# A two-block transformer kernel: constants and vectors ahead of the input, a 72-column slab with its weights stationary

## What is computed

```python
def first_block(x, c, norm_mix_g, w_in, ...):
    mod = silu(c) @ w_ada[l] + b_ada[l]
    sh_m, sc_m, g_m, sh_f, sc_f, g_f = jnp.split(mod, N_MOD, axis=-1)
    h = modulate(rmsnorm(x, norm_mix_g[l]), sh_m, sc_m)
    proj = h @ w_in[l]
    q, k, v, qi, ki, wi, u, ga, gb = jnp.split(proj, split_at, axis=-1)
    ...
    # dsa_attention, per block of queries
    idx_logits = jnp.einsum('btjd,bsd->btjs', qib, k_idx32) * (IDX_DIM ** -0.5)
    score = jnp.einsum('btj,btjs->bts', wb, jax.nn.relu(idx_logits))
    _, sel = lax.top_k(score, topk)
    ...
```

## Time and profile before

| | |
|---|---|
| median of three runs | 979.19 us |
| lowest, highest | 978.38, 985.32 us |
| the profiled execution | 981.8 us |
| its span, first to last instruction | 980.0 us |
| mean granted TensorE clock | 0.994 of full |
| PE, DVE, ACT busy | 95%, 64%, 47% of the span |

### The profile page before, as it was taken

The page is one execution under the profiler, slowest core; times in us unless marked ns, Lnnn a source line. Parts: engine busy times, 40 slices in busy tenths (PEclk is TensorE's granted clock), DMA queues, the critical chain, the costliest instruction groups (busy, mean ns, idle before and its releaser), DMA issues.

```text
span 980.0 us, 12127 instructions
## 1 busy us (share of the span) xinstructions
PE 932.3 (95%) x4313; PEld 749.4 (76%) x4313; DVE 629.6 (64%) x1020; ACT 458.5 (47%) x708; POOL 29.6 (3%) x41
## 2 busy tenths in 40 slices
PE   4799899999999999999999999999999999999997
PEld 4688664578878888887888777788788878888785
DVE  4478899988765555576766534578554565555444
ACT  1144432357364444453744554474455365555432
POOL 2100000000000000000000000000000000000000
PEclk9989999999999999999999999999999999999999
DMA  9977622584566565476565443146462456555531
GB/s 330 338 285 271 216 87 87 174 305 175 168 220 210 172 189 196 171 244 228 164 217 177 129 129 129 43 150 216 143 202 85 130 181 194 183 174 194 188 130 43
DMA packets 102999, 178.05 MB, mean 182 GB/s; under 512 B 6302, under 2 KB 52619, under 8 KB 102954
## 3 DMA queue, kind: packets, MB, share of 16 engines
q1 hardware_dynamic: 96138, 151.23, 46.9%
q0 software_dynamic: 6816, 26.22, 7.3%
HBM read 176.39 MB, written 1.05 MB: 181 GB/s over the span
## 4 chain that ended last, share of the span: by engine, by line
PE 81%; issue 7%; DVE 5%; DMA 3%; ACT 2%; SPq 0%; POOL 0%; DVEq 0%; POOLq 0%; ACTq 0%
PE bank L550 19%; PE bank L552 19%; PE bank L551 19%; PE bank L952 10%; PE bank L583 3%; DMA tap_rows<-in_w_dw 2%; DMA ada_raw<-in_w_ada 2%; PE bank L777 1%; ACT w_hi L1201 1%; DVE w_lo L1660 1%; PE bank L931 1%; PE bank L629 1%; PE bank L793 1%; PE bank L621 1%; PE bank L1146 1%
## 5 line engine op out<-in xcount | busy, mean ns | idle before, releaser
L1660 DVE TENSOR_TENSOR w_lo<-raw_weights,w_hi 128x1024 fp32r<-128x1024 f32 x267 | 324.4, 1222 | 241.5 <-ACT w_hi L1201 240.1
L1201 ACT ACTIVATE w_hi<-raw_weights 128x1024 fp32r<-128x1024 f32 x267 | 281.0, 1058 | 307.7 <-PE bank L552 230.0
L550 PE MATMUL bank<-w_hi,a_hi 128*128 128x512 f32 (+1 forms) x824 | 328.0, 398 | 5.9 <-DVE w_lo L1660 3.3
L552 PE MATMUL bank<-w_hi,a_lo 128*128 128x512 f32 (+1 forms) x824 | 321.0, 390 | 0.0
L551 PE MATMUL bank<-w_lo,a_hi 128*128 128x512 f32 (+1 forms) x824 | 320.6, 389 | 0.0
L550 PEld LDWEIGHTS bank<-w_hi,a_hi 128*128 128x128 f32 x824 | 155.6, 189 | 43.4 <-issue 7.3
L552 PEld LDWEIGHTS bank<-w_hi,a_lo 128*128 128x128 f32 x824 | 155.7, 189 | 32.7
L551 PEld LDWEIGHTS bank<-w_lo,a_hi 128*128 128x128 f32 x824 | 155.9, 189 | 29.9 <-issue 0.2
L952 PE MATMUL bank<-w_hi,ff_hi 128*128 128x512 f32 x176 | 55.1, 394 | 0.8 <-DVE hidden_rows L2162 0.5
L952 PE MATMUL bank<-w_lo,ff_hi 128*128 128x512 f32 x176 | 54.3, 389 | 0.0
L952 PE MATMUL bank<-w_hi,ff_lo 128*128 128x512 f32 x176 | 54.2, 389 | 0.0
(11 more groups left out here) (260 smaller groups left out, 867.4 us busy)
## 6 DMA issues: line engine op xcount, KB each, us to landing
raw_weights<-in_w_in SPq DMA_DIRECT2D x40, 1024.0 KB, 5.1
raw_weights<-in_w_ffn_in SPq DMA_DIRECT2D x44, 512.0 KB, 4.7
raw_weights<-in_w_gate_up SPq DMA_DIRECT2D x44, 512.0 KB, 4.3
ada_raw<-in_w_ada POOLq DMA_DIRECT2D x10, 1024.0 KB, 7.7
ada_start<-in_w_ada POOLq DMA_DIRECT2D x10, 1024.0 KB, 11.5
raw_weights<-in_w_ffn_out SPq DMA_DIRECT2D x9, 1024.0 KB, 4.9
raw_weights<-in_w_down SPq DMA_DIRECT2D x9, 1024.0 KB, 4.9
raw_weights<-in_w_out SPq DMA_DIRECT2D x8, 1024.0 KB, 5.1
```

What stands on the lines that cost most here:

```text
L550: pe.matmul(ps, hi[:, kt, ts], wh, start=start, stop=False)
L552: return pe.matmul(ps, lo[:, kt, ts], wh, start=False, stop=stop)
L1201: act.activation(w_hi[:, slot, 0:m], raw[:, b % RAW, half * PIECE:half * PIECE + m], ACT.Copy)\
L1660: dve.tensor_tensor(w_lo[:, slot, 0:m], raw[:, b % RAW, half * PIECE:half * PIECE + m], w_hi[:, slot, 0:m], ALU.subtract).then_inc(lo_read ...
```

## The change

- SP issues the constants, the eleven vectors and the taps right behind c, and only then waits for ada block 1 and issues x.
- PE transposes the vectors after the first two of its four column batches, and waits there for the constants and the small transfers; its other two column batches and the first sums come behind. DVE copies them out after ada block 2 instead of 6.
- The small slab is computed the other way round: weights stationary (72 columns), activations streaming (256 columns), 24 matmuls instead of 48, into one bank as 72 rows x 256 tokens.
- ACT copies this straight into rows 0 to 71 of kiT. Rows 0 to 63 are the transposed keys. POOL copies them to rows 64 to 127 by a transfer within the chip, which overwrites the weights' rows 64 to 71 once PE has transposed those back into bank 4 (two tiles of 8 columns). DVE scales them from there, as the last thing of slab (1, 3).
- ki_twice, its four copies, two large transposes and one copy of 256 columns are gone.

```diff
@@ SP @@
         sp.dma_start(c_cols[:], ...)
-        sp.wait_ge(*ada_signal(1))
-        sp.dma_start(x[:], ...).then_inc(sem["x_landed"], 16)
         ...
         sp.dma_start(tap_rows[:], ...).then_inc(small_landed, 16)
+        sp.wait_ge(*ada_signal(1))
+        sp.dma_start(x[:], ...).then_inc(sem["x_landed"], 16)
@@ POOL @@
         pool.wait_ge(nt["lo"], 4 * F_OF[N_H1] + 4)
-        for n in range(12, 20):
+        for n in range(12, 14):
+            ada_block(n)
+        pool.wait_ge(sem["wi_turned"], 1)
+        pool.dma_start(kiT[DH:2 * DH, :], kiT[0:DH, :]).then_inc(sem["ki_doubled"], 16)
+        for n in range(14, 20):
             ada_block(n)
@@ PE @@
-        for n in range(4):
+        for n in range(2):
             start_columns(n)
         pe.wait_ge(sem["const_landed"], 16)
-        start_sums(0)
-        start_sums(1)
         pe.wait_ge(small_landed, 16 * 12)
         ...
         last.then_inc(sem["vec_turned"], 1)
+        for n in range(2, 4):
+            start_columns(n)
+        start_sums(0)
+        start_sums(1)
         hold(5, 0)
@@ PE, small slab @@
-        for t in range(TT):
-            for kt in range(KD):
-                last = mm3(bank[2 * (U_SMALL % 2) + t][:, 0:SMALL], kt, t, a_hi, a_lo, sm_hi[:, kt, :],
-                           sm_lo[:, kt, :], kt == 0, kt == KD - 1)
-            if t == 0:
-                last.then_inc(acc_done, 1)
+        out = bank[2 * (U_SMALL % 2)][0:SMALL, 0:SEQ]
+        for kt in range(KD):
+            pe.matmul(out, sm_hi[:, kt, :], a_hi[:, kt, :], start=(kt == 0), stop=False)
+            before = pe.matmul(out, sm_lo[:, kt, :], a_hi[:, kt, :], start=False, stop=False)
+            last = pe.matmul(out, sm_hi[:, kt, :], a_lo[:, kt, :], start=False, stop=(kt == KD - 1))
+        before.then_inc(acc_done, 1)
@@ PE, slabs @@
                 if (s, j) == (1, 2):
-                    pe.wait_ge(sem["ki_copied"], 1)
                     for t in range(TT):
-                        last = pe.transpose(bank[4][:, t * P:(t + 1) * P], ki2[...], ident)
-                    last.then_inc(sem["ki_turned"], 1)
+                        pe.wait_ge(acc_free[t], U_SMALL + 1)
+                        last = pe.transpose(bank[4][:, t * HEADS:(t + 1) * HEADS], kiT[DH:SMALL, t * P:(t + 1) * P],
+                                            ident[DH:SMALL, DH:SMALL])
+                    last.then_inc(sem["wi_turned"], 1)
                 elif (s, j) == (2, 0):
-                    pe.wait_ge(sem["ki_moved"], 1)
+                    pe.wait_ge(sem["wi_scaled"], 1)
                 ...
                     pe.wait_ge(sem["qi_moved"], 2)
+                    pe.wait_ge(sem["ki_doubled"], 16)
                     logits(0, 3)
@@ ACT @@
-            act.wait_ge(*((piece_used, P_SMALL + 1) if t else (acc_done, U_SMALL + 1)))
-            act.activation(z[:, t, C_KI:C_U], bank[2 * (U_SMALL % 2) + t][:, 0:SMALL], ACT.Copy)\
+            act.wait_ge(piece_used, P_SMALL + 1)
+            act.activation(kiT[0:SMALL, t * P:(t + 1) * P], bank[2 * (U_SMALL % 2)][0:SMALL, t * P:(t + 1) * P], ACT.Copy)\
                 .then_inc(acc_free[t], 1)
         ...
-                if (s, k) == (1, 3):
-                    act.wait_ge(sem["ki_turned"], 1)
-                    act.activation(kiT[:], bank[4][:, 0:SEQ], ACT.Copy).then_inc(sem["ki_moved"], 1)
@@ DVE @@
-            elif n == 6:
+            elif n == 2:
                 dve.wait_ge(sem["vec_turned"], 1)
         ...
-                if (s, k) == (1, 0):
-                    ...
-                            last = dve.tensor_copy(ki2[:, t, c, :], z[:, t, C_KI:C_WI])
-                    last.then_inc(sem["ki_copied"], 1)
-                    dve.tensor_scalar(wi_s[:], z[:, :, C_WI:C_U], HEADS ** -0.5, None, ALU.mult)
+                if (s, k) == (1, 3):
+                    dve.wait_ge(sem["wi_turned"], 1)
+                    dve.tensor_scalar(wi_s[:], bank[4][:, 0:TT * HEADS].rearrange("p (t h) -> p t h", t=TT), HEADS ** -0.5,
+                                      None, ALU.mult).then_inc(sem["wi_scaled"], 1)
```

More of the change, by code:

```diff
@@ L213, in build @@
     kiT = sb("kiT", [P, SEQ])
-    ki2 = sb("ki_twice", [P, TT, 2, DH])
     u_at = region(24576)
@@ L381, in _ @@
         sp.dma_start(tap_rows[:], a["w_dw"].rearrange("o t i c -> (o t i) c")).then_inc(small_landed, 16)
+        sp.wait_ge(*ada_signal(1))
+        sp.dma_start(x[:], a["x"].rearrange("o (t p) d -> p (o t) d", p=P)).then_inc(sem["x_landed"], 16)
         def load(b, src, wide=None, i=0, step=0):
@@ L1339, in _ @@
                 conv(P_IN1 + 4 * s + 4 + k)
-                if (s, k) == (1, 3):
-                    act.wait_ge(sem["ki_turned"], 1)
-                    act.activation(kiT[:], bank[4][:, 0:SEQ], ACT.Copy).then_inc(sem["ki_moved"], 1)
-                elif (s, k) == (2, 2):
+                if (s, k) == (2, 2):
                     act.wait_ge(sem["pad_zeroed"], 1)
@@ L1917, in _ @@
                 conv(P_IN1 + 4 * s + 4 + k)
-                if (s, k) == (1, 0):
-                    dve.wait_ge(acc_free[0], U_SMALL + 1)
-                    dve.wait_ge(acc_free[1], U_SMALL + 1)
-                    for t in range(TT):
-                        for c in range(2):
-                            last = dve.tensor_copy(ki2[:, t, c, :], z[:, t, C_KI:C_WI])
-                    last.then_inc(sem["ki_copied"], 1)
-                    dve.tensor_scalar(wi_s[:], z[:, :, C_WI:C_U], HEADS ** -0.5, None, ALU.mult)\
-                        .then_inc(sem["wi_scaled"], 1)
+                if (s, k) == (1, 3):
+                    dve.wait_ge(sem["wi_turned"], 1)
+                    dve.tensor_scalar(wi_s[:], bank[4][:, 0:TT * HEADS].rearrange("p (t h) -> p t h", t=TT), HEADS ** -0.5,
+                                      None, ALU.mult).then_inc(sem["wi_scaled"], 1)
         dve.wait_ge(ada_step, ada_count(6))
```

3 lines of the change are left out of this document (removed).

## The result

The changed kernel takes 972.24 us, the median of seven runs (970.53 to 975.5). The kernel before, in seven runs beside it, has a median of 983.68 (978.38 to 985.32). These seven fall into two groups, two at 978.4 and 979.2 and five from 982.6 to 985.3, so the quotient of the two medians, 0.9884, says little; the ratio recorded for these runs is 0.9913, with a 95% interval of 0.9886 to 0.994: about 0.9% faster. The time lies inside the range, but the gain is a third smaller than forecast. The profiled execution took 972.24 us with a span of 970.3, so 9.6 us less than the profiled one of before, where the sum said 13.2.

What follows compares the result with a forecast made beforehand. TensorE, busy 932.3 of 980.0 us, was taken as the bound. Terms 9.3 + 4.9 = 14.2, less 1.0 for DMA collisions, left 13.2: 981.8 - 13.2 = 968.6, or 966.0 by the runs' median (2.6 lower); range 961 to 974.

Steps and rivals of the forecast that it cites:

- S: At the start: the time at which all twelve small transfers have landed, taken as 15 us, bounds 13.4 and 22.7.
- The list at half pace: TensorE's column batches, sums and transposes at the start, at their present pace: last sum at S + 21.6 = 36.6 us.
- part A: Start of the kernel: constants, vectors and taps issued ahead of x; gain 9.3 us, bounds 1.6 to 10.9.
- the clock rises early: Rival at the start: TensorE reaches 34.7 us, part A gives 11.2, time 964 us; chance 0.12.
- the vectors land late: Rival at the start: S is 19 to 22.7, part A shrinks to 5.3 to 1.6, time 970 to 974; chance 0.15.
- The floor: At the start: modulation block 7, landing near 31.4 us, allows the last column sum to end at 34.7.
- The slab: The 72-column slab: 24 matmuls in 2.8 us, gain 2.9; half-speed stretch behind it gone, 3.4; transposes 0.2.
- PE's wait for index_weights: Before the gate's reduction: 1.6 us of TensorE's gain in part B turns into a wait for VectorE's index_weights.
- part B: The reversed slab and what follows up to the gate: TensorE wants 6.5 us, VectorE allows 4.9; gain 4.9.
- the transfers bound the stretch from 45 to 70: Rival between 45 and 70 us: weight blocks come late for VectorE, 4 to 6 us, time 969 to 971; chance 0.15.
- the idle slice: Argument against the transfers rival: in the kernel before, the DMA engines stand still in 50 to 52 us.
- The far side: Rival at the start: small transfers land no sooner, S = 32; 3.3 us slower, 982.5; chance 0.03.

Runs made afterwards that it cites:

- hold_ada: The changed kernel, with GpSimd issuing modulation blocks 2 to 7 only once all twelve small transfers have landed; median 973.83 us, ratio 0.9938.
- after_5: The changed kernel repeated without edits, in a later group of runs; median 973.18 us, ratio 0.9929.
- queue_only: The changed kernel with TensorE's and VectorE's old order at the start, the small transfers still issued ahead of x; median 973.15 us, ratio 0.9907.
- warm: gate_late plus eight 256-column matmuls that compute nothing, where TensorE waits for the taps; median 970.01 us, ratio 0.9885.
- short48: gate_late plus 48 matmuls of 72 columns behind the slab, into a bank nobody reads; one run, 980.66 us.
- b_only: The changed kernel with part A taken back, so part B alone; median 977.64 us, ratio 0.9969.
- gate_late: The changed kernel with TensorE's gate reduction, and its wait for index_weights, one piece later; median 967.92 us, ratio 0.9897.
- gate_late_5: The same kernel as gate_late, measured again in more rounds beside the changed kernel; median 968.84 us, ratio 0.9881.
- after_again: The changed kernel repeated without edits, in another group of runs; median 971.14 us, ratio 0.9899.
- behind: The changed kernel, with weight blocks 7 and 8 issued only once modulation blocks 10 and 11 have landed; median 970.92 us, ratio 0.9925.
- a_only: The kernel before with part A alone, the 72-column slab as before; median 971.8 us, ratio 0.9924.
- lighter: The changed kernel, with late constants moved ahead of weight block 8 and the gate bias behind modulation block 11; median 973.22 us, ratio 0.993.

## Why the prediction was right or wrong

**S, the landing of the small transfers.** Taken at 15, measured 18.8 (18.4 to 19.4 in the other profiles with the early loads). Of the two bounds, 13.4 and 22.7, the lower was chosen because the queue is empty ahead of them. The text had the rows against this in its own hand, the 9 packets beside 203. The packets of the taps give the pace, and it would have dated S: 31 of 2 KB, one after the other, 0.25 us apart beside the big blocks (from 10.55 to 17.87 in the changed kernel) and 0.08 apart in hold_ada once blocks 0 and 1 are in. hold_ada shows the lower bound was real (12.7) but needs the big blocks held back. The rule cited there from the Trainium skill ("DMA: Bandwidth & Descriptors", section "Issuing engines are not separate DMA queues"), that transfers from different engines interleave on the same DMA engines, told in the right direction.

**The list at half pace.** The last sum was to end at S + 21.6. In the changed kernel's profile it ends at 36.86, almost the 36.6 of the text, but by two errors that cancel: S was 3.8 late, and the clock came up at 29.5 in the middle of the list. In after_5, where it came up late, the last sum ended at 39.8, against 18.9 + 21.6 = 40.5 by the rule. So the formula held, and the clock was the unknown. Nine profiles have this list (those with part A, without queue_only, hold_ada and warm): their first piece lies between 39.86 and 43.66. The two with the old start have 49.40 and 47.19. Part A is worth 9.5 us at the first piece in one pair of profiles and 3.5 in the least favourable. The rival "the clock rises early" came true and, but for 0.2 us, so did "the vectors land late" (19 to 22.7); the text had given them as alternatives. That the first piece met the forecast is luck.

**The floor.** Block 7's landing was to allow a last sum at 34.7. DVE sums blocks 4 to 7 without a pause from 23.29 until 35.29 in the changed kernel, so the floor is 36.2 (35.29 and a last sum of 0.95), set by DVE. This was not in the text; it is why warm could have given little even with the clock up.

**The slab.** 24 matmuls at 0.117, 2.82 us: right. No stretch at 0.50 behind it: right, and short48 shows the cause that the text had only supposed, in one execution. Its size was 2.5 instead of 3.6, transposes included: from the slab's end to the gate is 16.71 before and, without the wait, 14.21 now. The text halved all 6.8 us, though 0.9 of them lay within the old slab, which had its own term; that makes 0.5 of the missing 1.1, and the rest was not followed.

**PE's wait for index_weights.** Forecast 1.6, measured 1.39 in b_only, where part B stands alone, and 3.50 with both parts. The mechanism was right; it was worked out for part B alone.

**The sum.** This is the step that failed: 9.3 + 4.9 were added, and 1.0 taken for the transfers. With part A in place DVE gets block 10 at 61.1 to 62.3 in every profile in which it waits for it and the order of these transfers is kept, whether the first piece starts at 39.9 or 43.7. From there DVE has 10.1 to 10.2 us of work up to index_weights where the scaling stands at its new place; in after_5, queue_only, gate_late, gate_late_5 and warm a second wait, for block 11, adds 0.6 to 1.8. That keeps the gate from starting before about 72, and part A alone has it at 73.17. Of part B's 4.0 us some 0.8 are left at the gate. The forecast took modulation blocks 10 and 11 as landed and allowed 0.9 for them in part B. Measured were waits of 0.82 and 1.34 with part B alone (b_only) and 4.36 for block 10 with both parts. The rival "the transfers bound the stretch from 45 to 70", with a chance of 0.15 and a time of 969 to 971 (measured 972.24), is what happened; its stretch was right and its transfer was not: what comes late is no weight block but a modulation block. The argument against it, the idle slice, told of room at the old pace only: in 0 to 60 us the kernel before moves 18.1 MB and the changed one 20.9, from 32 us on at 374 to 392 GB/s without a gap. It does have one gap, from 28 to 30 us with 92 GB/s, which no run here tried to fill.

**The end.** The text let everything behind 110 us move with the stream, and listed a saving lost before the end among the things that would prove it wrong. It moved with it until 776 us, then 1.6 were lost to a half-speed stretch. That isn't the change's doing: after_again, the same kernel, has two such stretches elsewhere and takes 881.2 us from the logits to the end, where 878.2 is usual.

**The balance.** At the gate 11.45 instead of 13.2. Part A gave 9.54 in this pair instead of 9.3, part B 4.0 alone instead of 4.9, and with both in place 1.9, so that adding them cost 2.1 where 1.0 was allowed: 1.75 short in all. Then 1.6 for the stretch at 777 and 0.25 in between and at the end make 13.2 - 9.6 = 3.6. The other 2.6 us between 966.0 and 972.24 is the step by which the profiled time was lowered to the median of three runs: 979.19 was that median, but the runs of before reach from 976.8 to 985.6, so neither value was firm to 2.6 us. Nor was the gain of 9.6 between the two profiles. Over all groups the kernel before has 49 runs with a lowest of 976.77 and a median of 979.46, the changed one 18 with 970.51 and 972.22: 6.3 and 7.2 us. The profile that the forecast started from is an execution with a late clock (42.3) and 6.8 us at half speed behind the slab. The fastest of the kernel before has a span of 975.0, which by the 878.1 us from its logits to the end leaves an estimated 96.9 for the head, 5.0 less than in that profile. Which of the two accounts for it is open, since only one execution of that kernel has a trace.

**The rest.** The transfer within the chip was hidden, as costed: it landed 7 us after its issue at 72, and the logits at 90.6 did not wait. The far side (small transfers not sooner at all) did not occur.

## What to carry to other kernels

Gains of two edits add only if the same resource isn't next behind both: look for the first transfer that is due after each edit, and ask what else is in flight with it then, not how far it lay ahead of its consumer in the old profile. A transfer that waited for nothing before can be the limit once two edits have moved its consumer. Where a wait is found, ask first what stands behind it that needs nothing from it; moving one converted piece ahead of the gate gave more than both edits to the transfers. Before a term goes into the sum as one number, look at several executions of it: with one list at the start the first piece lay anywhere within 3.8 us here, mostly by the clock. The distance from the logits to the end, which came out the same within 0.3 us in six profiles, tells where to look.

## What the runs showed of the hardware

The granted clock differs between executions of the same instructions. It came up between 29.5 and 36.7 us with one list. In warm the column batches and transposes did not keep it up: it fell at 21.1, and PE had been busy without a pause since 19.24, behind one of 0.68 us. In these profiles the stretches at 0.50 before the end lasted 3.4 or 6.8 us, 10.2 in short48 and 13.7 in warm. Behind the logits their cost can be read from the 878.0 to 878.3 us without them or with one at 135 to 152: nothing that shows for the 3.4 us in the kernel before at 148, in after_5 at 138 and in behind at 135, where DVE is busy 1.8 to 2.0 of every 2 us and PE pauses; 1.2 for the 6.8 us in hold_ada at 140; 1.5 to 1.7, half of the length, for each one from 542 us on (short48, with 2.8 us for one, apart). What stands before such a stretch is thin work on PE. That was the stream of 72-column matmuls in the kernel before, in a_only and in short48, the one-column matmuls in warm, and otherwise a pause of 1.3 to 3.6 us, as in these windows of after_again:

```profile
540.00:542.00 2.00, 0.73 (x3) 1.00 0.00 0
542.00:544.00 2.00, 2.00 (x6) 0.52 0.39 85
```

A pause brings it only sometimes: PE's 3.50 us at the gate did not in the changed kernel, 3.28 did in lighter. The Trainium skill, "TensorE: Matmul & The Clock Gate", section "HAM oscillation — how this bites in real kernels", blames pauses between bursts of matmuls for such falls. The trace points the same way for after_again, where a pause of 1.36 us stands before the fall (busy 0.73 of 2.00), and goes further in the earlier trace rows and short48, where PE is busy 1.00 throughout and the clock falls all the same. What decides between two executions of the same kernel stays open.

Of the twelve small transfers the last, the taps, takes 12.8 us from its issue at 6.0 to its landing beside six more blocks of 1 MB, and 7.0 from 5.76 in hold_ada, where two such blocks are in flight. The packets in the traces show why. In hold_ada from 10 to 11 us, with no block in flight, the taps move alone at 25 GB/s, and the DMA share is 0.06, one sixteenth: the packets of this transfer, one per row, go one at a time, each in 0.08 us. Beside the blocks they start 0.25 us apart, which is one packet of the taps (0.09) and one of 4 KB of a block (0.16). Its 31 rows make 31 packets, and these take 7.3 us beside the blocks and 2.5 alone. The Trainium skill, "DMA: Bandwidth & Descriptors", section "Queues, rings and completion order", says that a DMA engine takes turns between its queues packet by packet. The trace agrees: one packet of the taps each 0.25 us makes 8 in the 2 us of the earlier trace rows, which has 9, and the 203 beside them are those of all sixteen engines.
